# Delta rule's inversion: the second token tile in the other half of the partitions, two heads at a time

## The reference, cut to what matters

```
kb = kc * bc[..., None]
a_mat = jnp.where(strict, jnp.einsum("bnhid,bnhjd->bnhij", kb, kc) * gamma, 0.0)
lhs = a_mat + jnp.eye(c, dtype=a_mat.dtype)
rhs = jnp.concatenate([vc * bc[..., None], kb * jnp.exp(decay)[..., None]], axis=-1)
sol = lax.linalg.triangular_solve(lhs, rhs, left_side=True, lower=True, unit_diagonal=True)
u, w = sol[..., :dv], sol[..., dv:]
```

## Time and profile before

| | |
|---|---|
| median of 3 runs | 832.42 us |
| the profiled execution's own time | 832.43 us |
| its span | 830.7 us |
| PE busy | 814.1 us, 98% of the span, 5444 matmul records |
| DVE busy | 602.4 us, 73% |
| ACT busy | 445.7 us, 54% |
| POOL busy | 118.8 us, 14% |
| mean granted TensorE clock | 1.000 |

### The profile page before, as it was taken

The page is one execution under the profiler, slowest core; times in us unless marked ns, Lnnn a source line. Parts: engine busy times, 40 slices in busy tenths (PEclk is TensorE's granted clock), DMA queues, the critical chain, the costliest instruction groups (busy, mean ns, idle before and its releaser), DMA issues.

```text
span 830.7 us, 13387 instructions
## 1 busy us (share of the span) xinstructions
PE 814.1 (98%) x5444; PEld 707.8 (85%) x5444; DVE 602.4 (73%) x901; ACT 445.7 (54%) x665; POOL 118.8 (14%) x141
## 2 busy tenths in 40 slices
PE   8999999999999999999989999999999999999998
PEld 6988867998898888888879899888798888888886
DVE  4579787846788878877876999985767577666662
ACT  4466735653667666656564666354454455444440
POOL 0136000110000000000012989610010000000000
PEclk9999999999999999999999999999999999999999
DMA  9975435543554765565423625110423357655521
GB/s 307 326 238 203 149 140 182 173 169 119 185 176 156 241 215 170 186 208 198 161 93 108 204 88 167 52 42 12 149 85 121 127 184 275 226 191 179 189 101 51
DMA packets 92633, 135.90 MB, mean 164 GB/s; under 512 B 4467, under 2 KB 76795, under 8 KB 92444
## 3 DMA queue, kind: packets, MB, share of 16 engines
q1 hardware_dynamic: 90572, 129.72, 46.5%
q10 hardware_dynamic: 1264, 2.70, 1.0%
q0 software_dynamic: 736, 2.63, 1.0%
HBM read 133.46 MB, written 1.06 MB: 162 GB/s over the span
## 4 chain that ended last, share of the span: by engine, by line
PE 76%; DVE 17%; ACT 3%; issue 2%; DMA 1%; POOL 0%; SPq 0%; ACTq 0%; DVEq 0%
PE acc L2315 26%; PE work L2315 14%; PE work L2340 14%; PE work L2343 7%; PE work L2288 3%; DVE split_operands L1528 3%; DVE arena L1843 2%; DVE split_extra_slot L1528 2%; DVE arena L1866 2%; PE work L2261 1%; PE work L3015 1%; PE work L2699 1%; DVE arena L1794 1%; PE work L2718 1%; PE work L2631 1%
## 5 line engine op out<-in xcount | busy, mean ns | idle before, releaser
L1528 DVE TENSOR_TENSOR split_operands<-weight_ring,split_operands 128x2048 fp32r<-128x2048 f32 x79 | 181.3, 2302 | 55.6 <-ACT split_operands L983 55.4
L2315 PE MATMUL acc<-split_operands 128*128 128x512 f32 x808 | 193.4, 391 | 0.2 <-DVE split_operands L2231 0.2
L983 ACT ACTIVATE split_operands<-weight_ring 128x2048 fp32r<-128x2048 f32 x79 | 150.2, 1909 | 54.1 <-PE acc L2315 23.7
L2315 PEld LDWEIGHTS acc<-split_operands 128*128 128x128 f32 x808 | 150.0, 188 | 31.2 <-issue 0.6
L2315 PE MATMUL work<-split_operands 128*128 128x256 f32 (+1 forms) x832 | 111.9, 291 | 1.0 <-DVE arena L1866 0.5
L2315 PEld LDWEIGHTS work<-split_operands 128*128 128x128 f32 x832 | 105.0, 191 | 6.0 <-issue 3.5
L2340 PE MATMUL work<-split_operands 128*128 128x512 f32 x400 | 99.8, 391 | 0.0
L1528 DVE TENSOR_TENSOR split_extra_slot<-weight_ring,split_extra_slot 128x2048 fp32r<-128x2048 f32 x35 | 81.3, 2322 | 19.3 <-ACT split_extra_slot L983 19.1
L970 ACT ACTIVATE arena<-work 128x512 f32<-128x512 f32 (+3 forms) x81 | 37.8, 475 | 90.8 <-PE work L2315 39.3
L2340 PEld LDWEIGHTS work<-split_operands 128*128 128x128 f32 x400 | 72.8, 189 | 13.6
L983 ACT ACTIVATE split_extra_slot<-weight_ring 128x2048 fp32r<-128x2048 f32 x35 | 66.8, 1907 | 23.2 <-DMA weight_ring<-in_w_in 11.7
(11 more groups left out here) (344 smaller groups left out, 1095.5 us busy)
## 6 DMA issues: line engine op xcount, KB each, us to landing
weight_ring<-in_mlp_w SPq DMA_DIRECT2D x32, 1024.0 KB, 5.2
weight_ring<-in_w_up SPq DMA_DIRECT2D x22, 1024.0 KB, 5.1
weight_ring<-in_w_in SPq DMA_DIRECT2D x20, 1024.0 KB, 5.8
weight_ring<-in_w_down SPq DMA_DIRECT2D x11, 1024.0 KB, 4.9
weight_ring<-in_w_out SPq DMA_DIRECT2D x8, 1024.0 KB, 4.8
weight_ring<-in_w_mk SPq DMA_DIRECT2D x4, 1024.0 KB, 5.0
weight_ring<-in_w_mv SPq DMA_DIRECT2D x4, 1024.0 KB, 5.6
weight_ring<-in_w_mq SPq DMA_DIRECT2D x4, 1024.0 KB, 5.4
```

The source lines that it names most:

```text
L983: act.activation(slot_of(u)[:, 0, :], weights(u, 2048), ACT.Copy).then_inc(high_ready, 1)
L1528: dve.tensor_tensor(slot[:, 1, :], weights(split_units[i], 2048), slot[:, 0, :], ALU.subtract).then_inc(low_ready, 1)
L2315: ins = pe.matmul(out, lhs(p), rhs(q), start=(start and n == 0), stop=(stop and n == 2))
```

## The change

The matmuls of tile 1 write to the other 64 partitions (`half ^ t`), so that rows 0 to 63 of the array go to partitions 64 to 127 and the reverse. Six levels exchange the halves six times, so the last result lies as before. The loop over tiles is inside that over heads: a level is done in two groups g of two heads, and in a group the matmuls of tile 0 and 1, half 0 and 1 follow each other. The narrow and the wide product of a group and tile lie in one bank, columns 0 to 127 and 128 to 383, named ("level", level, t, g); the list `tiles` has these in place of "y" and "w", with as many banks taken in total.

Since both readers use one bank, they take turns: of each group ACT copies tile 0 (`level_copied`) while DVE signs tile 1 (`level_signed`); then ACT copies tile 1, waiting for that sign, and DVE signs tile 0, waiting for that copy. The one increment of a bank comes from the later reader. A group of PE waits for both tiles of the same group of the level before. Level 0 now waits for both signs of "y" of level 0, and ACT's first copy for both unit diagonals. The order of all other work on each engine stays.

```diff
-    for level in range(LEVELS):
-        for t in range(TT):
-            if level < LEVELS - 1:
-                tiles.append(("y", level + 1, t))
-            tiles.append(("w", level, t))
+    tiles.extend(("level", n, t, g) for n in range(LEVELS - 1) for g in range(2) for t in range(TT))
+    tiles.extend(("w", LEVELS - 1, t) for t in range(TT))
...
             def inverse_steps(level):
-                for t in range(TT):
-                    name = ("w", level, t)
-                    if level == 0:
-                        act.wait_ge(unit_diag, t + 1)
-                    drain(name, pair_of[t], bank(name)[:, :].rearrange("p (h w i) -> p h w i", h=GDN_HEADS, w=2)
-                          ).then_inc(reader(name), 1)
+                for g in range(2):
+                    for t in range(TT):
+                        name = ("level", level, t, g)
+                        if t == 0:
+                            if level == 0:
+                                act.wait_ge(unit_diag, TT)
+                            act.wait_ge(*full(name))
+                        else:
+                            act.wait_ge(level_signed, 2 * level + g + 1)
+                        act.activation(pair_of[t][:, 2 * g:2 * g + 2, :, :],
+                                       bank(name)[:, P:P + SEQ].rearrange("p (h w i) -> p h w i", h=2, w=2), ACT.Copy
+                                       ).then_inc(reader(name) if t else level_copied, 1)
...
             def signed(level):
-                for t in range(TT):
-                    name = ("y", level, t)
-                    dve.wait_ge(*full(name))
-                    dve.tensor_tensor(step_s[level % 2][t], blocks_of(name),
-                                      signs[:, level, :].unsqueeze(1).broadcast_to([P, GDN_HEADS, CHUNK]), ALU.mult
-                                      ).then_inc(reader(name), 1)
+                for g in range(2):
+                    for t in (1, 0):
+                        name = ("level", level - 1, t, g)
+                        if t:
+                            dve.wait_ge(*full(name))
+                        else:
+                            dve.wait_ge(level_copied, 2 * level + g - 1)
+                        dve.tensor_tensor(step_s[level % 2][t][:, 2 * g:2 * g + 2, :],
+                                          bank(name)[:, 0:P].rearrange("p (h i) -> p h i", h=2),
+                                          signs[:, level, :].unsqueeze(1).broadcast_to([P, 2, CHUNK]), ALU.mult
+                                          ).then_inc(level_signed if t else reader(name), 1)
...
+            def level_products(level, g):
+                step = step_s[level % 2]
+                ps = [open_tile(("level", level, t, g)) for t in range(TT)]
+                for j in range(2):
+                    h = 2 * g + j
+                    for t in range(TT):
+                        for half in range(2):
+                            r, to = in_chunk(half), in_chunk(half ^ t)
+                            pe.matmul(ps[t][to, CHUNK * j:CHUNK * j + CHUNK], pair_of[t][r, h, 0, :], step[t][r, h, :],
+                                      start=True, stop=True)
+                for j in range(2):
+                    h = 2 * g + j
+                    for t in range(TT):
+                        for half in range(2):
+                            r, to = in_chunk(half), in_chunk(half ^ t)
+                            ins = pe.matmul(ps[t][to, P + P * j:P + P * j + P], step[t][r, h, :],
+                                            pair_of[t][r, h, :, :].rearrange("p w i -> p (w i)"), start=True, stop=True)
+                        if j:
+                            ins.then_inc(tile_full, 1)
...
             for level in range(LEVELS):
...
+                if level < LEVELS - 1:
+                    for g in range(2):
+                        if level:
+                            for t in range(TT):
+                                pe.wait_ge(*drained(("level", level - 1, t, g)))
+                        level_products(level, g)
...
+                    for h in range(GDN_HEADS):
+                        for t in range(TT):
+                            for half in range(2):
+                                r, to = in_chunk(half), in_chunk(half ^ t)
+                                ins = pe.matmul(ps[t][to, CHUNK * h:CHUNK * h + CHUNK], step[t][r, h, :], pair_of[t][r, h, 1, :],
+                                                start=True, stop=True)
+                            if h == GDN_HEADS - 1:
+                                ins.then_inc(tile_full, 1)
```

More of the change, by code:

```diff
@@ L481, in block_kernel @@
         unit_diag = sem("unit_diagonal_set")
+        level_copied = sem("level_first_tile_copied")
+        level_signed = sem("level_second_tile_signed")
         first_eye = sem("first_inverse_set")
@@ L2049, in signed @@
             def signed(level):
-                for t in range(TT):
-                    name = ("y", level, t)
-                    dve.wait_ge(*full(name))
-                    dve.tensor_tensor(step_s[level % 2][t], blocks_of(name),
-                                      signs[:, level, :].unsqueeze(1).broadcast_to([P, GDN_HEADS, CHUNK]), ALU.mult
-                                      ).then_inc(reader(name), 1)
-            signed(0)
+                for g in range(2):
[10 more added lines that the diff above has]
+            for t in range(TT):
+                name = ("y", 0, t)
+                dve.wait_ge(*full(name))
+                dve.tensor_tensor(step_s[0][t], blocks_of(name),
+                                  signs[:, 0, :].unsqueeze(1).broadcast_to([P, GDN_HEADS, CHUNK]), ALU.mult
+                                  ).then_inc(reader(name), 1)
             topk_rounds(1, TOPK_ROUNDS - 7)
@@ new lines, in _ @@
+            for t in range(TT):
+                pe.wait_ge(*drained(("y", 0, t)))
+                pe.wait_ge(first_eye, t + 1)
+            for level in range(LEVELS):
+                if level < LEVELS - 1:
+                    for g in range(2):
+                        if level:
+                            for t in range(TT):
+                                pe.wait_ge(*drained(("level", level - 1, t, g)))
+                        level_products(level, g)
+                else:
+                    for g in range(2):
+                        for t in range(TT):
+                            pe.wait_ge(*drained(("level", level - 1, t, g)))
+                    step = step_s[level % 2]
+                    ps = [open_tile(("w", level, t)) for t in range(TT)]
+                    for h in range(GDN_HEADS):
+                        for t in range(TT):
+                            for half in range(2):
[4 more added lines that the diff above has]
+                                ins.then_inc(tile_full, 1)
```

## The result

The changed kernel takes **839.03 us** (median of 6 runs, 836.74 to 840.68); the kernel before, on the same chip, 832.44 (6 runs, 832.22 to 833.95). The ratio is 1.0071 [1.0057, 1.0084]: slower by 6.6 us, where 2.6 were forecast. The profiled execution took 838.63 us with a span of 836.9 (before: 830.7, so +6.2).

The account below looks back on a forecast made before the run. PE and DVE were taken to share the limit, with DVE's and ACT's queues deciding. The inverse's copy moves from 558.44 to 561.05: 830.7 + 2.6 + 1.73 = 835.0 us, likeliest case 834.0 to 836.0, stated range 832.4 to 836.4.

Parts of the forecast that it names:

- The turns: ACT and DVE alternating on shared banks in the inversion's levels: stalls put the inverse's copy at 561.05, +2.6 us.
- signed(1): DVE's signs of level 0's products: start at 543.97 us as before, DVE going on at 545.15, was 544.63.
- signed(2): DVE's signs of level 1's products, after conv and maxima: start at 548.38 us, DVE going on at 549.56.
- ACT back: ACT free for level 2's copies after the first exponentials and table load: 552.41 us, where it was 550.93.
- signed(3): DVE's signs of level 2's products: begin 551.04 us, the second piece waiting for ACT until 552.41; DVE on at 553.51.
- signed(5): DVE's signs ahead of PE's last level: start at 558.93 us, end 560.19, PE's last level starting 560.24.
- the hand-over to PE: PE's start after the sign or copy it waits for, in each level: taken as 0.05 us.
- The four corners: PE's products in the levels: four corners run side by side, a half level streaming in 0.67 us.
- so it comes through whole: Chain after the inverse's copy: no wait found that absorbs the delay, so all +2.6 us reach the total.
- the lower clock: Rival: PE's waits lower its clock, products from 559.35 to 564.50 take up to twice as long; 836.5 to 840 us, chance 0.06.
- PE as the bound: Rival in the levels: PE was the bound and the turns cost no stall; -1.3, 831.2 us, chance 0.10.
- Nothing of the delay was given back: Rival: part of the delay is taken back, +0.5 to +1.6 us remaining, 833.5 us; chance 0.17.

Follow-up runs that it names:

- e2: Kernel before with four corners, narrow and wide products in banks of their own, whole tiles of four heads, no turns: median 834.45 us, ratio 1.0007.
- e5: The changed kernel again, unaltered, on the second chip: median 837.87 us, ratio 1.0073 to the kernel before.
- e7: Changed kernel with products that nobody uses behind levels 0 to 2 only: median 837.62 us, ratio 1.0063 to the kernel before.
- e8: Kernel before with one pause: PE waits ahead of its last level for five POOL memsets; median 837.46 us, ratio 1.0066.
- e6: Changed kernel with products that nobody uses behind levels 3 and 4 only: median 835.73 us, ratio 1.0036 to the kernel before.
- e3: Changed kernel with 31 products that nobody uses, behind levels 0 to 4: median 835.91 us, ratio 1.0030 to the kernel before.
- e1: Changed kernel, but tile 1's matmuls stay in tile 0's two corners: median 837.41 us, ratio 1.0044 to the kernel before.
- e4: Changed kernel, but ACT copies tile 0 of all heads before tile 1: median 835.24 us, ratio 1.0030 to the kernel before.
- e10: Kernel before with four corners, own banks, no turns, plus five unused products behind each of levels 3 and 4: median 832.94 us, ratio 0.9999.
- e9: Changed kernel, ACT copying tile 0 of all heads first, plus 6 and 9 unused products behind levels 3 and 4: median 834.71 us, ratio 1.0020.

## Why the prediction was wrong

**The turns: right.** The steps of the sum came where they were put: signed(1) 543.89 (543.97 forecast), DVE on at 545.10 (545.15), signed(2) 548.34 (548.38), the table load 549.60 (549.56), ACT back at 552.45 (552.41), signed(3) from 550.92 (551.04) and waiting 1.64 for that, level 3's copies 555.62 (555.63), signed(5) 558.96 (558.93). The work order around each wait and the durations (128 columns in 0.29 us, 0.38 for ACT) were enough for this, because DVE and ACT were the bound all along; e2 shows that from the other side.

**One term mis-sized: the hand-over to PE.** I took 0.05, from level 0. The same trace has 0.14 at level 1, in the chain of the kernel before:

```profile
...
544.05 0.34 DVE arena L2053
...
544.53 2.90 PE work L3015 x64
...
```

In the changed kernel PE starts a half level 0.14 behind ACT's copy, which it waits for last (544.21 and 0.39 in the chain, to 544.73), and the last level 0.32 behind the end of the last sign (559.97 + 0.29 to 560.58). That put the inverse's copy at 561.36 instead of 561.05 (with a start 0.08 earlier), and the cost of the turns at 3.0 instead of 2.6. Of the difference 0.27 is the last hand-over; the rest, about 0.1, had gathered in the steps up to the last sign.

**The four corners: right, and worthless.** Half a level streams in 0.72 us (544.73 to 545.45; 0.67 forecast). The Trainium skill ("TensorE: Matmul & The Clock Gate", "Wait — 56ns, not 53.3ns?") has starts never closer than about 25 ns; 16 narrow records pass in 0.26 us here, 16 ns each. For products in four corners the trace disagrees with that rule.

**The step that failed: "so it comes through whole".** More came through than the delay. I named the lower clock, and its place for one of the two low stretches ("the products from 559.35 to 564.50 ... up to twice"), and then gave it 0.06, because the longest wait before was 1.8 us and no row showed the clock behind a longer one. That is no evidence against it, least of all where the forecast itself makes PE wait up to 2.5 us. In 18 runs of the changed kernel and of the kernels that keep its pause (after, e5, e7) not one kept a clock of 1.00. One low stretch in part B costs 1.35 to 1.64 (e7 30.16, e2 30.36, e5 30.40 and e8 30.45, for 28.81); two cost 3.2 in the profiled execution. That the time of 839 us lies in the rival's own 836.5 to 840 is in part luck: the second stretch, at 576 to 580, was in no part of the forecast. The median is 6.6 over before. Of that 3.0 are the turns, and the other 3.6 are put down to the clock, since of those runs only the profiled one could be divided (3.0 and 3.2). On the second chip, where e6 ran beside it, taking out the two late waits was worth 837.87 - 835.73 = 2.1 of 5.4.

The Trainium skill (same page, "A second HAM failure mode: psum-queue depth-cycling") says that a PE which idles briefly between groups of products, while banks go round, swings between the two clocks. The traces agree, with 0.67 behind the early waits of e6 and 0.70 behind the late ones of e7, and e8 adds that one pause will do.

**The rivals.** PE as the bound is refuted by e2. Nothing of the delay was given back: A and B add up to the span. Where the clock is held the change costs near to what was forecast: e3 and e6 stand 3.1 and 3.3 us over before by the fastest runs (835.33 and 835.40 against 832.19 and 832.13).

**What stays open.** Why the first profile has a second low stretch in part B (576 to 580) and that of e5 none, though PE had been busy for 10 us there; why the levels of the first profile and of e6 have one and those of e5 none behind the same waits; and why on the first chip the kernel before falls as well (17 of its 32 runs stood at 0.996 to 0.998). So what e1, e2 and e4, with shorter waits, lose to the clock is not shown to come from their waits. Low stretches come elsewhere too, at 50 to 60 us in the profile of e10 (0.72, then 0.94) and at 585 to 595 in that of e9 (0.95, then 0.71); a run's mean clock alone does not say where it fell. Ahead of the products with the inverse PE also waits 1.01 us for its copy; this wait is in e3, e6 and e9 as well, whose clock holds there, so it does not lower it by itself. The 2.1 us of turns that e4 leaves are placed by the trace (1.04 before the table load, the rest behind ACT), not taken apart on the chip.

## What to carry to other kernels

Before speeding up the engine with the highest busy share, follow the queues of the others through the same stretch: here two strict queues set the time of every level, and putting both readers of a result into one bank made each wait for the other at a place where it had been free to run ahead. A wait that the change gives TensorE is not free just because the engine was not the bound: ask what clock the products behind it will get, and above all those on the critical path right after. If such a wait can't be avoided, products that nobody uses, behind the last useful ones, can cost less than the lower clock does: those of e6 cost nothing in A, and its median is 2.1 us below that of e5.

## What the runs showed of the hardware

- The granted clock fell after PE had resumed, and not in the pause: in e8 PE resumed at 560.78, and windows of 1 us give 1.00 from 561, 0.91 from 562, 0.50 from 563 to 566 and 0.88 from 566. That low stretch of 3.4 us cost 1.6, with PE full from 563 on. The delay differs: 2.0 us in e8; 2.5 in the changed kernel behind its last wait (PE from 560.58, and 0.55 in the window from 563); 0.3 there behind the wait ahead of level 2 (PE from 549.18, and 0.72 in the window from 549).
- The mean granted clock of a run counts such stretches. By an estimate from e8, 3.4 us at half the clock in 837 us are 0.002, so the 0.998 to 0.992 of the changed kernel's runs would be one to four of them.
- 64x64 products in four corners: 16 ns a record at 64 columns (0.26 us for 16), and in two corners 0.03 us.
- PE's start behind the end of what it waited for last: 0.05 us at level 0 and 0.14 at level 1 of the kernel before, 0.14 at a half level and 0.32 ahead of the last level of the changed kernel. What makes the difference no run took apart.
